# Moving activations of the split float32 products kept in two planes, the second 64 bytes off modulo 128

## What is computed

```python
def hybrid_layer(h, w_in, ...):
    proj = h @ w_in                       # 256 x 2048 by 2048 x 12320
    ...                                   # delta rule and attention, per head
    return jnp.concatenate([y_a, y_b], axis=-1) @ w_out

def shortconv_layer(h, w_in, conv_w, w_out):
    gate_b, gate_c, u, z = jnp.split(h @ w_in, 4, axis=-1)
    y = gate_b * causal_depthwise_conv(gate_c * u, conv_w)
    return (y * jax.nn.silu(z)) @ w_out
```

## Time and profile before

| | |
|---|---|
| median of 3 runs | 3014.7 us (3014.14 to 3017.23) |
| the profiled execution, its time | 3016.94 us |
| its span in the trace | 3015.2 us |
| mean granted TensorE clock | 0.994 |
| TensorE busy with matmuls | 2949.6 us (98%) |
| weight loads | 2567.2 us (85%) |
| VectorE, ScalarE, GpSimd busy | 72%, 50%, 15% |
| DMA | 209 GB/s on average |

### The profile page before, as it was taken

The page is one execution under the profiler, slowest core; times in us unless marked ns, Lnnn a source line. Parts: engine busy times, 40 slices in busy tenths (PEclk is TensorE's granted clock), DMA queues, the critical chain, the costliest instruction groups (busy, mean ns, idle before and its releaser), DMA issues.

```text
span 3015.2 us, 51441 instructions
## 1 busy us (share of the span) xinstructions
PE 2949.6 (98%) x17510; PEld 2567.2 (85%) x17510; DVE 2158.2 (72%) x3030; ACT 1505.2 (50%) x2164; POOL 452.3 (15%) x187
## 2 busy tenths in 40 slices
PE   7999999999999999999999999999999999999998
PEld 6889999889988888888887877788887888888887
DVE  6666666766668888888887889876687436565466
ACT  4454444444444444444444777766544444444443
POOL 0111011110100000000000000000002445545443
PEclk9999999999999999999999999999999999999999
DMA  6443434444457887888875454456785566766655
GB/s 213 145 139 132 133 131 141 144 134 143 150 191 262 313 293 279 315 304 305 297 290 197 163 169 168 165 193 214 245 301 181 190 207 223 244 237 236 207 182 175
DMA packets 172691, 629.42 MB, mean 209 GB/s; under 512 B 19224, under 2 KB 20376, under 8 KB 171808
## 3 DMA queue, kind: packets, MB, share of 16 engines
q1 hardware_dynamic: 165024, 601.99, 57.1%
q10 hardware_dynamic: 7552, 25.91, 2.5%
HBM read 615.22 MB, written 12.60 MB: 208 GB/s over the span
## 4 chain that ended last, share of the span: by engine, by line
PE 68%; issue 25%; DVE 4%; ACT 2%; DMA 1%; DVEq 0%; SPq 0%; POOL 0%; ACTq 0%; POOLq 0%
PE gemm L537 41%; PE gemm L542 20%; PE side L678 1%; DVE wl L1528 1%; PE side L685 1%; ACT wh L984 1%; PE side L690 1%; DMA raw<-in_stream 1%; PE side L563 0%; DVE xs L1617 0%; DMA x<-in_x 0%; PE side L745 0%; DVE gB L1729 0%; ACT gA L1086 0%; PE side L722 0%
## 5 line engine op out<-in xcount | busy, mean ns | idle before, releaser
L537 PE MATMUL gemm<-xs,wh 128*128 128x512 f32 x5120 | 1646.0, 403 | 25.1 <-DVE stage L1533 7.3
L984 ACT ACTIVATE wh<-raw 128x1024 fp32r<-128x1024 f32 x939 | 984.2, 1057 | 925.3 <-PE gemm L542 806.2
L1528 DVE TENSOR_TENSOR wl<-raw,wh 128x1024 fp32r<-128x1024 f32 x811 | 1034.2, 1279 | 445.5 <-ACT wh L984 426.1
L542 PEld LDWEIGHTS gemm<-xs,wl 128*128 128x128 f32 x5120 | 965.3, 189 | 226.0
L542 PE MATMUL gemm<-xs,wl 128*128 128x256 f32 x5120 | 1011.8, 279 | 0.0
L537 PEld LDWEIGHTS gemm<-xs,wh 128*128 128x128 f32 x5120 | 783.2, 189 | 54.1 <-issue 47.0
L537 PE MATMUL gemm<-hid,wh 128*128 128x512 f32 x2368 | 747.6, 397 | 6.6 <-DVE fxg L1533 2.2
L542 PEld LDWEIGHTS gemm<-hid,wl 128*128 128x128 f32 x2368 | 446.9, 189 | 100.9
L542 PE MATMUL gemm<-hid,wl 128*128 128x256 f32 x2368 | 468.6, 279 | 0.0
L1457 POOL TENSOR_TENSOR wl<-raw,wh 128x1024 fp32r<-128x1024 f32 x128 | 349.0, 2732 | 368.5 <-ACT wh L984 368.5
L537 PEld LDWEIGHTS gemm<-hid,wh 128*128 128x128 f32 x2368 | 357.5, 188 | 9.4 <-ACT wh L984 3.2
(11 more groups left out here) (385 smaller groups left out, 1964.0 us busy)
## 6 DMA issues: line engine op xcount, KB each, us to landing
raw<-in_stream SPq DMA_DIRECT2D x940, 512.0 KB, 4.0
ada_a<-in_ada SPq DMA_DIRECT2D x144, 512.0 KB, 5.1
ada_b<-in_ada SPq DMA_DIRECT2D x48, 512.0 KB, 5.1
stash<-stage ACTq DMA_DIRECT2D x12, 512.0 KB, 3.6
att<-stash ACTq DMA_DIRECT2D x8, 384.0 KB, 4.3
x<-in_x SPq DMA_DIRECT2D x4, 512.0 KB, 5.6
xacc<-in_x ACTq DMA_DIRECT2D x1, 2048.0 KB, 11.6
stash<-stA ACTq DMA_DIRECT2D x4, 512.0 KB, 6.8
```

The source lines that it names most:

```text
L537: mm(G[n][:, :], wh[:, slot, at:at + P], rhs(sl * SLAB_K + k), start=sl == 0 and k == 0, stop=False, skip_group_check=True)
L542: op = mm(G[n][:, T:2 * T], wl[:, slot, at:at + P], rhs(sl * SLAB_K + k)[:, 0:T], start=False, stop=last, skip_group_check=True)
L984: A(wh[:, slot, :], raw[:, slot, :], ACT.Copy).then_inc(hi_ready, 1)
L1528: tt(wl[:, slot, :], raw[:, slot, :], wh[:, slot, :].bitcast(F32), ALU.subtract).then_inc(lo_ready[slot], 1)
```

## The change

The moving tiles are kept in two planes: `xs` is now [128, 2, 16*256+16] and `hid` [128, 2, 24*256+16]; plane 0 holds the low parts of all chunks, plane 1 the high parts. A plane of `xs` is 4112 values or 16448 bytes long, which is 128 times 128 plus 64, so that the high plane begins 64 bytes off modulo 128. `hid2` is kept as two halves of 16 chunks with two planes each. A matmul of 512 columns now reads two runs of 1024 bytes, the low one first; one of 256 columns reads one run in the high plane. The place of `hid` is moved up so that it equals that of `xs` modulo 512 (and with it 0 modulo 128). The order of the matmuls, the weights and the PSUM columns that each instruction writes stay as they are; since the low part is streamed first, columns 0 to 255 of a bank now hold wh by xl, and 256 to 511 the two products with xh. The copies and subtractions that write the tiles address the planes, other tiles are moved to make room (`yg`, `fsum`, the tiles over the upper half of `hid2`, the ring of the `ada` tiles), and the gate product's sums are read with their halves exchanged. No wait, no instruction and no transfer is added or taken away in the source.

```diff
+GAP, LO, HI = 16, 0, 1
-    xs = place("xs", [P, KC, 2 * T], F32R)
+    xs = place("xs", [P, 2, KC * T + GAP], F32R)
+    top[0] += (xs_at - top[0]) % 512
     hid_at = top[0]
-    hid = place("hid", [P, 24, 2 * T], F32R)
+    hid = place("hid", [P, 2, 24 * T + GAP], F32R)
-    hid2 = nc.alloc_sbuf_tensor_at("hid2", [P, 32, 2 * T], F32R, offset=hid_at)
+    hid2 = nc.alloc_sbuf_tensor_at("hid2", [P, 2, 2, 16 * T + GAP], F32R, offset=hid_at)
+    def xs_part(part, k, n):
+        return chunks_of(xs[:, part, k * T:(k + n) * T], n)
...
-                        op = mm(G[n][:, T:2 * T], wl[:, slot, at:at + P], rhs(sl * SLAB_K + k)[:, 0:T], start=False,
+                        op = mm(G[n][:, T:2 * T], wl[:, slot, at:at + P], rhs(sl * SLAB_K + k)[:, HI, :], start=False,
                                 stop=last, skip_group_check=True)
...
         def xs_of(k):
-            return xs[:, k, :]
+            return xs[:, :, k * T:(k + 1) * T]
...
         def hid_of(chunks):
-            return lambda k: hid[:, chunks[k], :]
+            return lambda k: hid[:, :, chunks[k] * T:(chunks[k] + 1) * T]
+        def hid2_of(first):
+            return lambda k: hid2[:, (first + k) // 16, :, (first + k) % 16 * T:((first + k) % 16 + 1) * T]
...
-            o, y = xs[:, 2 * s:2 * s + 2, 0:T], norm_y_buf[n][:, 2 * (s % 2):2 * (s % 2) + 2, :]
+            o, y = xs_part(HI, 2 * s, 2), norm_y_buf[n][:, 2 * (s % 2):2 * (s % 2) + 2, :]
...
-            hi, lo = xs[:, 2 * s:2 * s + 2, 0:T], xs[:, 2 * s:2 * s + 2, T:2 * T]
+            hi, lo = xs_part(HI, 2 * s, 2), xs_part(LO, 2 * s, 2)
...
-                low(hid[:, bass.ds(2 * it, 2), T:2 * T], yv2, hid[:, bass.ds(2 * it, 2), 0:T]
+                low(hid_part(LO, 2 * it, 2), yv2, hid_part(HI, 2 * it, 2)
                     ).then_inc(S("ya_lo"), 1)
```

More of the change, by code:

```diff
@@ L144, in program, with chunks_of, hid_part, hid2_part @@
     xacc = nc.alloc_sbuf_tensor_at("xacc", [P, KC, T], F32, offset=xs_at)
+    def chunks_of(ap, n):
+        return ap.rearrange("p (n t) -> p n t", n=n)
+    def xs_part(part, k, n):
+        return chunks_of(xs[:, part, k * T:(k + n) * T], n)
+    def hid_part(part, k, n):
+        return chunks_of(hid[:, part, k * T:(k + n) * T] if isinstance(k, int) else hid[:, part, bass.ds(k * T, n * T)], n)
+    def hid2_part(part, k, n):
+        if isinstance(k, int):
+            return chunks_of(hid2[:, k // 16, part, k % 16 * T:(k % 16 + n) * T], n)
+        return chunks_of(hid2[:, 0, part, bass.ds(k * T, n * T)], n)
     def V(name, a=0, n=None):
@@ L283, in program @@
     rr = place("rr", [P, 2, T])
[L284 to L287 removed]
+    assert top[0] <= arena2, (top[0] - hid_at)
+    top[0] = free_lo
     mSb = place("mSb", [P, 384])
@@ L613, in gates @@
                 for k in range(KC):
-                    op = mm(ps0[:, :], wab2[:, k, :], xs[:, k, :], start=(k == 0), stop=(k == KC - 1))
+                    op = mm(ps0[:, :], wab2[:, k, :], xs_of(k), start=(k == 0), stop=(k == KC - 1))
                 op.then_inc(S("gate_pe"), 1)
@@ L619, in gates @@
                     o = ps1[:, 32 * c:32 * c + 32]
-                    mm(o, gsum[0:64, c * P:(c + 1) * P], H("sel")[0:64, :], start=True, stop=False,
+                    mm(o, gsum[0:64, T + c * P:T + (c + 1) * P], H("sel")[0:64, :], start=True, stop=False,
                        skip_group_check=True)
-                    op = mm(o, gsum[0:32, T + c * P:T + (c + 1) * P], H("sel")[0:32, :], start=False, stop=True,
+                    op = mm(o, gsum[0:32, c * P:(c + 1) * P], H("sel")[0:32, :], start=False, stop=True,
                             skip_group_check=True)
@@ L808, in _ @@
         for i in range(4):
-            group(G_SCOUT + i, Q_SCOUT + 3 * i, 12, lambda k: hid[:, k, :], sc_ready,
+            group(G_SCOUT + i, Q_SCOUT + 3 * i, 12, hid_of(range(24)), sc_ready,
                   at_slot(21, lambda: earlier(2)) if i == 3 else None)
@@ L922, in _ @@
         for i in range(4):
-            group(G_MRG + i, Q_MRG + i, 4, lambda k: hid2[:, 8 + k, :], att_in)
+            group(G_MRG + i, Q_MRG + i, 4, hid2_of(8), att_in)
         def mrg_ready(sl):
@@ L929, in _ @@
         for i in range(4):
-            group(G_WO + i, Q_WO + 2 * i, 8, lambda k: hid2[:, 16 + k, :], mrg_ready,
+            group(G_WO + i, Q_WO + 2 * i, 8, hid2_of(16), mrg_ready,
                   at_slot(13, lambda: earlier(3)) if i == 3 else None)
@@ L943, in ff_out @@
         def ff_out(c, i, hook=None):
-            group(G_FF + 8 * c + 4 + i, Q_FF + 16 * c + 8 + 2 * i, 8, lambda k: hid2[:, k, :], ff_ready(c), hook)
+            group(G_FF + 8 * c + 4 + i, Q_FF + 16 * c + 8 + 2 * i, 8, hid2_of(0), ff_ready(c), hook)
         with pe.Fori(0, 2) as i2:
@@ L1111, in delta @@
                 act.wait_ge(S("ya"), it + 1)
-                A(hid[:, bass.ds(2 * it, 2), 0:T], yh[:, :, :].rearrange("p j i -> p (j i)"), ACT.Copy
+                A(hid_part(HI, 2 * it, 2), yh[:, :, :].rearrange("p (v c) i -> p v (c i)", v=2), ACT.Copy
                   ).then_inc(S("ya_hi"), 1)
@@ L1131, in attn @@
                 act.wait_ge(S("yb"), it + 1)
-                A(hid[:, 16 + it, 0:T], yb[:, :], ACT.Copy).then_inc(S("yb_hi"), 1)
+                A(hid_part(HI, 16 + it, 1), yb[:, :].unsqueeze(1), ACT.Copy).then_inc(S("yb_hi"), 1)
         def heads(it):
@@ L1186, in sc_round @@
             act.wait_ge(S("sc_y"), j + 1)
-            A(hid[:, 4 * j:4 * j + 4, 0:T] if isinstance(j, int) else hid[:, bass.ds(4 * j, 4), 0:T],
+            A(hid_part(HI, 4 * j, 4),
               yv[:, :, :], ACT.Copy).then_inc(S("sc_hi"), 1)
@@ L1251, in gelu @@
                 act.wait_ge(S("m_yg"), QK_HEADS + j + 1)
-                A(hid2[:, 16 + j, 0:T], uT[:, j, :], ACT.Copy).then_inc(S("m_hi"), 1)
+                A(hid2_part(HI, 16 + j, 1), uT[:, j:j + 1, :], ACT.Copy).then_inc(S("m_hi"), 1)
         def before_ssm(slot):
@@ L1328, in glu @@
                 act.wait_ge(S("glu_y"), i + 1)
-                A(hid2[:, 4 * i:4 * i + 4, 0:T], uT[:, 4 * i:4 * i + 4, :], ACT.Copy).then_inc(S("glu_hi"), 1)
+                A(hid2_part(HI, 4 * i, 4), uT[:, 4 * i:4 * i + 4, :], ACT.Copy).then_inc(S("glu_hi"), 1)
         def keep_late(n):
@@ L1385, in moba @@
                     act.wait_ge(loads["stash"], 16 * 12)
-                A(hid2[:, 8 + h, 0:T], ps3[:, 0:T], ACT.Copy).then_inc(S("t_hi"), 1)
+                A(hid2_part(HI, 8 + h, 1), ps3[:, 0:T].unsqueeze(1), ACT.Copy).then_inc(S("t_hi"), 1)
         for n, (q, count) in enumerate(ATT_GROUPS):
@@ L1414, in _ @@
             act.wait_ge(S("mrg"), i + 1)
-            A(hid2[:, 16 + 4 * i:20 + 4 * i, 0:T], smm[i % 2][:, :, :], ACT.Copy, scale=0.5).then_inc(S("mrg_hi"), 1)
+            A(hid2_part(HI, 16 + 4 * i, 4), smm[i % 2][:, :, :], ACT.Copy, scale=0.5).then_inc(S("mrg_hi"), 1)
         for i in range(4):
@@ L1423, in ff_in @@
             act.wait_ge(S("ff"), 4 * c + i + 1)
-            A(hid2[:, 4 * i:4 * i + 4, 0:T] if isinstance(i, int) else hid2[:, bass.ds(4 * i, 4), 0:T],
+            A(hid2_part(HI, 4 * i, 4),
               mt[:, :, :], ACT.Copy).then_inc(S("ff_hi"), 1)
@@ L1817, in attn @@
                 dve.wait_ge(S("yb_hi"), it + 1)
-                low(hid[:, 16 + it, T:2 * T], yb[:, :], hid[:, 16 + it, 0:T]).then_inc(S("yb_lo"), 1)
+                low(hid_part(LO, 16 + it, 1), yb[:, :].unsqueeze(1), hid_part(HI, 16 + it, 1)).then_inc(S("yb_lo"), 1)
         def heads(it):
@@ L1950, in sc_round @@
                     dve.wait_ge(S("sc_hi"), j + 1)
-                    o = hid[:, 4 * j:4 * j + 4, :] if isinstance(j, int) else hid[:, bass.ds(4 * j, 4), :]
-                    low(o[:, :, T:2 * T], yv[:, :, :], o[:, :, 0:T]
+                    low(hid_part(LO, 4 * j, 4), yv[:, :, :], hid_part(HI, 4 * j, 4)
                         ).then_inc(S("sc_lo"), 1)
@@ L2110, in gelu @@
                 dve.wait_ge(S("m_hi"), QK_HEADS + j + 1)
-                low(hid2[:, 16 + j, T:2 * T], uT[:, j, :], hid2[:, 16 + j, 0:T]).then_inc(S("m_lo"), 1)
+                low(hid2_part(LO, 16 + j, 1), uT[:, j:j + 1, :], hid2_part(HI, 16 + j, 1)).then_inc(S("m_lo"), 1)
         def ssm(slot):
@@ L2165, in glu @@
                 dve.wait_ge(S("glu_hi"), i + 1)
-                low(hid2[:, 4 * i:4 * i + 4, T:2 * T], uT[:, 4 * i:4 * i + 4, :], hid2[:, 4 * i:4 * i + 4, 0:T]
+                low(hid2_part(LO, 4 * i, 4), uT[:, 4 * i:4 * i + 4, :], hid2_part(HI, 4 * i, 4)
                     ).then_inc(S("glu_lo"), 1)
@@ L2198, in moba @@
                 dve.wait_ge(S("t_hi"), h + 1)
-                tt(hid2[:, 8 + h, T:2 * T], ps3[:, 0:T], hid2[:, 8 + h, 0:T].bitcast(F32), ALU.subtract
+                tt(hid2_part(LO, 8 + h, 1), ps3[:, 0:T].unsqueeze(1), hid2_part(HI, 8 + h, 1).bitcast(F32), ALU.subtract
                    ).then_inc(S("t_lo"), 1)
@@ L2269, in ff_in @@
             dve.wait_ge(S("ff_hi"), 4 * c + i + 1)
-            o = hid2[:, 4 * i:4 * i + 4, :] if isinstance(i, int) else hid2[:, bass.ds(4 * i, 4), :]
```

(2 more changed lines are left out.)

27 lines of the change are left out of this document (15 added, 12 removed).

## The result

The changed kernel takes 3022.93 us (median of 8 runs, 3020.36 to 3026.28) against 3014.76 us for the kernel before in the same series (8 runs, 3013.01 to 3017.23). The ratio is 1.0025 with a 95% interval of 1.0015 to 1.0034: slower by about 8 us, 0.25%, just over the 0.2% that the prediction called distinguishable. The forecast was 3006.0 us, faster.

What follows compares the result with a forecast made beforehand. A stream of matmuls with few holes was taken to bound the kernel, so round length counts; 3014.7 - 8.7 us for the moving reads, other terms 0, gave 3006.0 us, range 2965 to 3045 us.

Steps and rivals of the forecast that it cites:

- What bounds the kernel: Whole kernel: matmul stream with few holes; only the round length, 3744 rounds, moves time by more than a few us.
- The contention of the two reads: In each round: distance between moving operand and weights modulo 128 counts; 64 off is 3.4 ns a round shorter.
- its own sign of being wrong: In the round: wl matmuls (L542) or the gap from wl to next wh changing would mean the contention's place misread.
- Step 1, the moving reads: Moving reads of each round: every round becomes like hid's, 8.7 us gained; bounds 4.0 us lost, 62.7 us gained.
- The seam, step 2: 512-column matmuls reading two runs 16448 bytes apart instead of one: taken as 0, bounded above by 89.9 us.
- Rival C: 512-column wh matmuls: reads of the same half in a row hold each other up, 25.5 us, 3040 us; chance 0.28.
- Rival B: Round length: nothing or the average, 3010.1 to 3018.7 us; separate read ports would give 3014.7 us; chance 0.28.
- Steps 3 and 4: ScalarE and VectorE tile writes: counted nothing, address work at most 4.0 us; moved tiles: no wait added, 0.

Runs made afterwards that it cites:

- the exchange: The kernel before with xs at 64 and hid at 0 modulo 128, their places exchanged against the kernel before; 3009.53 us (one run).
- the gap of 0: The changed kernel with a gap of 0 values in place of 16, both planes at 0 modulo 128; 3016.11 us, ratio 1.0006.

## Why the prediction was wrong

**What bounds the kernel** was right: the waits stayed (32.4 us against 32.5), and the time moved with the length of the round.

**The contention of the two reads** was right as far as it went. The distance of the moving chunk from the weights sets the round, and not tile, stage or absolute place (weights moved, the exchange). The prediction had it as a distance modulo 128 and the first and second tile's difference as its size; the runs fit a period of 256 and show a gain of 6.7 ns at +64 where hid, at -64, had shown 3.4. Where it sits was read wrongly. The prediction took from the durations, whose ends are modelled, that the 256-column matmuls have no part in it, and named its own sign of being wrong: that L542 or the gap from wl to the next wh changes. That sign came. With xs the part of the round from the wl pair to the next wh pair grew by 3.9 ns, and the part in front of it became 2.0 ns shorter.

**Step 1, the moving reads, is the step that failed.** It took a round with two kinds of reads to lie between the rounds with one kind, and bounded it by 0.6933 and 0.6967 us. No row showed a mixed round, and the prediction said so, but its bounds weren't bounds: the mixed round takes 0.6987 us in both tiles, outside both (all but the 160 rounds on the second half of `hid2`). It forecast 8.7 us gained, and about 8 us were lost. With the other mixtures it is 0.7022 (high at 0, low at 64), 0.7000 or 0.7067 (two distances to wh and wl), 0.7200 (low at -64, high at 0), and 0.6869 or 0.7000 (low at 64, high at 128). Being mixed was worth -3 to +23 ns against the nearer of its own two ends, and an average of shares has no meaning here.

**The alignment of hid** was in the text of the change and in step 1 only as a share. By itself it costs 3.3 ns a round, 0.6933 to 0.6967, as the exchange and the gap of 0 show; 1184 x 3.3 ns = 3.9 us of the loss. The 64 bytes between the planes then add 2.0 ns to each round of both tiles, 3744 x 2.0 = 7.5 us. The sum of 11.4 us overstates the 8.2 us, since it counts all rounds: those without side work or a wait make 8.5 us.

**The seam, step 2,** costs 0 where it is only a break into two runs, shown at distances 0 and 64. But the seam that step 2 described has its upper half behind an upper half, and this is the same 64 bytes that mix the distances. In that form its 0 fell together with step 1, and no run parts the two. That mixing alone can cost, without any seam, shows with wl moved. Rival C had the right sign by a mechanism that the runs allow only in part. What separates gap 16 from gap 0 is that the upper half of 128 bytes follows the upper half, as C had it; but its price isn't fixed. The same step costs 2.0 ns from a low run at 0 and gives 3 ns back in one rhythm from a low run at 64. Its 25 us came from the 3.4 ns between two unmixed rounds, a row that doesn't price a mixed one.

**Rival B's rule** from the Trainium skill, TensorE: Matmul & The Clock Gate, step-by-step section, that the moving operand and LDWEIGHTS have separate read ports, doesn't cover what is seen. Moving wl by 64 bytes lengthens the round by 10 ns with the moving reads unchanged.

**Steps 3 and 4** (writers, address work, moved tiles) hold: no wait of TensorE grew by more than 0.7 us, and the address work in front of the subtractions is what it was (31 times 105 ns, 19 times 40 ns).

Two things stay open. The mechanism by which the distance acts isn't in any trace; that a weight load and a moving read collide is argued from the places that matter, not shown. Against one rival, the writes into the weights by the other engines, the hid stretch of the kernel before speaks. VectorE writes `wl` for 1.2 us and ScalarE `wh` for 1.1 us of every four rounds there, and yet each of 121 rounds takes 692 to 695 ns. And what picks the rhythm where there are several wasn't tried.

## What to carry to other kernels

When a stream of matmuls fills the span, measure the round start to start in the timeline and compare tiles with different addresses: a few ns a round are visible there and nowhere else, and moving xs by 64 bytes and hid by 128 was worth 12 us here, where a new layout lost 8. Vary the distance between moving operand and weights as a whole, over 256 bytes, and keep it the same for all reads of a round, unless a measured mixture is better. Look at several stretches, as one layout can run in more than one rhythm. Don't interpolate between two steady rhythms: a mixture can lie outside both, so an edit that mixes them isn't bounded by the two.

## What was not expected of the hardware

Rounds of 1536 columns at full clock took 0.6869 to 0.7200 us with the same number and order of matmuls, by the places of the operands and the rhythm that a stretch is in, and 0.640 us would be the columns' own time. They settle into exact cycles: one round of 0.6933 us, five rounds in 3.49 us, or 0.7200 us with every matmul of a kind at the same 403 or 283 ns.
